# One Strassen level for the gate and up products of a decoder layer, with block sums by DMA and the hidden activations through HBM

## The reference, cut to what matters

```python
def channel_and_ple(h, p, g_ffn, w_gate, w_up, w_down, g_ple, w_ple_gate, w_ple_proj):
    n = rms_norm(h, g_ffn)
    h = h + (jax.nn.silu(n @ w_gate) * (n @ w_up)) @ w_down
    gate = jax.nn.sigmoid(rms_norm(h, g_ple) @ w_ple_gate)
    return h + gate * (p @ w_ple_proj)
```

## Time and profile before

| what | value |
|---|---|
| three timed runs | 2737.95, 2739.5, 2742.2 us; median 2739.5 |
| the profiled execution: first to last instruction | 2738.2 us |
| its own time (span plus 1.3 us, taken as the median of the runs less its span) | 2739.5 us |
| gate and up, four chunks | 255.84 + 253.70 + 253.69 + 253.70 = 1016.93 us |
| down, four chunks | 126.71 + 126.72 + 126.72 + 126.71 us |
| read through SP's DMA queue | 224.95 MB |

### The profile page before, as it was taken

How to read it: one execution, slowest core, us unless ns; L and a number is a source line. 1 busy time by engine, 2 the same in 40 slices (tenths; PEclk the granted TensorE clock), 3 DMA queues, 4 the chain that set the end, 5 groups by cost and what they waited for, 6 DMA issues and landing times. The chain is left out here.

```text
span 2738.2 us, 53856 instructions
## 1 busy us (share of the span) xinstructions
PE 2691.1 (98%) x21924; PEld 2652.9 (97%) x21924; DVE 1288.0 (47%) x1632; ACT 757.9 (28%) x1024; POOL 274.8 (10%) x279
## 2 busy tenths in 40 slices
PE   6999999999999999999999999999999999999998
PEld 6999999999999999999999999999999999999998
DVE  6557665666585553334333334333334333456332
ACT  3223332333242232222222222222222222233221
POOL 5201111111121410000000000000000000043001
PEclk8999999999999999999999999999999999999999
DMA  5733333333334323322323323333223333233332
GB/s 143 220 107 94 100 104 110 102 100 104 108 110 135 93 85 92 92 82 86 108 84 92 92 82 89 106 92 92 85 82 100 93 92 92 79 90 100 102 107 61
DMA packets 467782, 272.81 MB, mean 100 GB/s; under 512 B 17926, under 2 KB 456746, under 8 KB 467208
## 3 DMA queue, kind: packets, MB, share of 16 engines
q1 hardware_dynamic: 443216, 224.95, 28.4%
q0 software_dynamic: 20768, 43.38, 5.2%
q10 hardware_dynamic: 3744, 3.74, 0.5%
HBM read 259.11 MB, written 17.22 MB: 101 GB/s over the span
## 5 line engine op out<-in xcount | busy, mean ns | idle before, releaser
L390 PE MATMUL acc<-xhi,whi 128*128 128x260 f32 x5376 | 1103.0, 286 | 10.1 <-DVE xlo L969 7.3
L394 PE MATMUL acc<-xhi,wlo 128*128 128x260 f32 x5376 | 1089.1, 284 | 0.0
L392 PE MATMUL acc<-xlo,whi 128*128 128x260 f32 x5376 | 1087.3, 284 | 0.0
L961 DVE TENSOR_TENSOR wlo<-wraw,whi 128x1024 fp32r<-128x1024 f32 x468 | 577.4, 1234 | 968.1 <-ACT whi L705 962.2
L390 PEld LDWEIGHTS acc<-xhi,whi 128*128 128x128 f32 x5376 | 835.3, 190 | 20.1 <-DVE xlo L969 8.6
L394 PEld LDWEIGHTS acc<-xhi,wlo 128*128 128x128 f32 x5376 | 834.8, 190 | 0.0
L392 PEld LDWEIGHTS acc<-xlo,whi 128*128 128x128 f32 x5376 | 834.1, 190 | 0.0
L705 ACT ACTIVATE whi<-wraw 128x1024 fp32r<-128x1024 f32 x468 | 495.0, 1058 | 1176.4 <-PE acc L394 1093.3
L394 PE MATMUL acc<-fhi,wlo 128*128 128x260 f32 x1408 | 283.4, 283 | 0.0
L390 PE MATMUL acc<-fhi,whi 128*128 128x260 f32 x1408 | 283.3, 282 | 0.0
L392 PE MATMUL acc<-flo,whi 128*128 128x260 f32 x1408 | 283.2, 282 | 0.0
(11 more groups left out here) (214 smaller groups left out, 1489.9 us busy)
## 6 DMA issues: line engine op xcount, KB each, us to landing
wraw<-in_w_in SPq DMA_DIRECT2D x96, 512.0 KB, 3.8
wraw<-in_w_gate SPq DMA_DIRECT2D x88, 512.0 KB, 3.7
wraw<-in_w_up SPq DMA_DIRECT2D x88, 512.0 KB, 3.7
wraw<-in_w_down SPq DMA_DIRECT2D x64, 384.0 KB, 3.3
wraw<-in_w_down SPq DMA_DIRECT2D x64, 320.0 KB, 3.1
wraw<-in_w_out SPq DMA_DIRECT2D x32, 512.0 KB, 3.8
wraw<-in_w_ple_gate SPq DMA_DIRECT2D x32, 512.0 KB, 3.9
kv<-in_cache_k POOLq DMA_DIRECT2D x8, 1024.0 KB, 7.2
```

The lines of the kernel that those rows point to most:

```text
L390: mm(acc[:, slot, h, 0:HALF], w_h, hi[:, kt, h * HALF:(h + 1) * HALF], start=begin, stop=False)
L392: mm(acc[:, slot, h, 0:HALF], w_h, lo[:, kt, h * HALF:(h + 1) * HALF], start=False, stop=False)
L394: done = mm(acc[:, slot, h, 0:HALF], w_l, hi[:, kt, h * HALF:(h + 1) * HALF], start=False, stop=end)
L961: V.tensor_tensor(wlo[:, u % HILO, :], wraw[:, u % RAW, :], whi[:, u % HILO, :].bitcast(F32), ALU.subtract).then_inc(s_wlo, 1)
```

## The change

Gate and up: for a pair of hidden tiles the weight of each matrix is cut in 2x2 blocks (even or odd block of the model width, first or second hidden tile), and the data in 2x2 blocks (even or odd tile, first or second half of the tokens). Seven products of block sums (Winograd's form) take the place of eight. Each of the 44 matrix and tile-pair combinations ("pair" below, `PAIRS`) is 7 units of 24 matmuls (8 blocks by 3 matmuls, 260 columns). Of the four weight sums, DVE adds two (`block_sum`), and two are made by a DMA that POOL issues and that adds HBM data to a buffer (`add_blocks`, `accum_op`). The block buffers are single (`block_11`, `block_21`, `block_12`, `sum_1`, `sum_2`), only `block_22` is double. The seven data blocks of each of 8 tile pairs are made once (`parts_added`, `parts_hi`, `parts_lo`); those of the last four lie on the memory of the attention operand and of `hid`, so `hid` is first stored to HBM (`h_dram`). PSUM results are combined by DVE, ACT and POOL (`corner`). Each finished pair of hidden tiles is stored to HBM (`f_dram`).

Down: only after all of gate and up, in 4 passes over 4, 14, 15 and 11 hidden tiles that are loaded back (`load_hidden`); the first pass adds the stored `h_dram` tiles, which come through the two tiles of `res`. `transpose_p` moves to the last pass.

```diff
-CHUNK = 11
-CHUNKS = D_FF // P // CHUNK
-DOWN = (6, 5)
+KP2 = KT // 2
+EARLY = KP2 // 2
+FT = D_FF // P
+PAIRS = FT
+TURN = 4
+DOWN = ((4,), (7, 7), (8, 7), (6, 5))
...
@@ SP
+        def block_pair(i, first=False, last=False):
...
+                    sp.wait_ge(s_sum, i * 4 + 2 * e)
+                    sp.sem_inc(s_freed, 1)
+                block(block_21, w, 1, 0, i * (2 * P), l_21)
...
+                    sp.wait_ge(s_wlo, i * 14 + (U_G + 7 * e - 7 + 3))
+                    sp.sem_inc(s_freed, 1)
+                block(block_12, w, 0, 1, i * (2 * P), l_12)
+                if not fresh:
+                    sp.wait_ge(s_wlo, i * 14 + (U_G + 7 * e - 7 + 6))
+                    sp.sem_inc(s_freed, 1)
+                    block(block_11, w, 0, 0, i * (2 * P), l_11)
...
@@ PE
+        def gate_up(at, it, r, fresh=False):
...
+                pe.wait_ge(s_wlo, at.count(w))
...
+                to = bank(BANK_OF[u])
+                for p in range(KP2):
+                    if first and u == 0:
+                        pe.wait_ge(s_xp, p + 1)
+                    hi, lo, n = x_parts(p)
+                    w_h = whi[:, w % HILO, p * P:(p + 1) * P]
+                    w_l = wlo[:, w % HILO, p * P:(p + 1) * P]
+                    mm(to, w_h, hi[:, n, X_OF[u], :], start=p == 0, stop=False)
+                    mm(to, w_h, lo[:, n, X_OF[u], :], start=False, stop=False)
+                    done = mm(to, w_l, hi[:, n, X_OF[u], :], start=False, stop=p == KP2 - 1)
...
+        pe.wait_ge(l_f[0], 16)
...
+        with pe.Fori(1, KT // 4) as i:
+            for b in range(4):
+                pe.wait_ge(s_read, i * 4 + (T_D + b - 1))
+                unit(Span(U_D, 4, i), b, *down_units(0, 0), b % 2, True, True)
...
@@ ACT
+        def block_hi(at, it, r, v):
...
+            elif v == 5:
+                act.wait_ge(l_sum3, nn * 16 + 16)
...
+            act.wait_ge(s_unit, at.count(w) - HILO)
+            on(whi[:, w % HILO, :], source, ACT.Copy).then_inc(s_whi, 1)
...
+        def parts_hi(p):
...
+            on(hi[:, n, 0, :], hid[:, 2 * p, 0:HALF], ACT.Copy, scale=cols[:, g0:g0 + 1])
+            on(hi[:, n, 1:3, :], halves(hid[:, 2 * p + 1, :]), ACT.Copy, scale=cols[:, g0 + 1:g0 + 2])
+            act.wait_ge(s_parts, 4 * p + 4)
+            on(hi[:, n, 3:6, :], parts[p % 2][:, 0:3, :], ACT.Copy)
+            on(hi[:, n, 6, :], parts[p % 2][:, 3, :], ACT.Copy, scale=-1.0).then_inc(s_xphi, 1)
...
+        act.wait_ge(s_unit, U_G)
+        for p in range(EARLY, KP2):
+            parts_hi(p)
+            if p + 2 < KP2:
+                half_scaled(p + 2)
...
@@ DVE
+        def block_sum(at, it, r, n, fresh):
...
+            if n == 2:
+                dve.wait_ge(l_11, nn * 16 + 16)
+                dve.wait_ge(s_wlo, at.count(7 * r - 1))
+                dve.wait_ge(s_sum, it * 8 + (2 * r + 1))
+                out, a, b = sum_2, sum_1, block_11
+            V.tensor_tensor(out, a, b, ALU.add).then_inc(s_sum, 1)
...
+        def block_lo(at, r, v):
...
+            source = (block_11, sum_2, block_12, sum_1, block_22(r), block_11, sum_2)[v]
+            dve.wait_ge(s_whi, at.count(w))
...
+        def parts_added(p):
...
+            V.scalar_tensor_tensor(to[:, 1, :], hid[:, 2 * p, 0:HALF], g0, half, ALU.mult, ALU.subtract
+                                   ).then_inc(s_parts, 1)
+            V.scalar_tensor_tensor(to[:, 3, :], hid[:, 2 * p + 1, HALF:T], g1, half, ALU.mult, ALU.subtract
+                                   ).then_inc(s_parts, 1)
+            dve.wait_ge(s_parts, 4 * p + 1)
+            V.scalar_tensor_tensor(to[:, 0, :], hid[:, 2 * p + 1, HALF:T], g1, to[:, 1, :], ALU.mult, ALU.add
+                                   ).then_inc(s_parts, 1)
+            dve.wait_ge(s_parts, 4 * p + 3)
+            V.scalar_tensor_tensor(to[:, 2, :], hid[:, 2 * p + 1, 0:HALF], g1, to[:, 0, :], ALU.mult, ALU.subtract
+                                   ).then_inc(s_parts, 1)
...
+        def parts_lo(p):
...
+            V.scalar_tensor_tensor(lo[:, n, 0, :], hid[:, 2 * p, 0:HALF], g0, hi[:, n, 0, :].bitcast(F32),
+                                   ALU.mult, ALU.subtract)
+            V.scalar_tensor_tensor(lo[:, n, 1:3, :], halves(hid[:, 2 * p + 1, :]), g1, hi[:, n, 1:3, :].bitcast(F32),
+                                   ALU.mult, ALU.subtract)
+            V.tensor_tensor(lo[:, n, 3:6, :], parts[p % 2][:, 0:3, :], hi[:, n, 3:6, :].bitcast(F32), ALU.subtract)
+            V.scalar_tensor_tensor(lo[:, n, 6, :], parts[p % 2][:, 3, :], -1.0, hi[:, n, 6, :].bitcast(F32),
+                                   ALU.mult, ALU.subtract).then_inc(s_xp, 1)
...
+        for p in range(EARLY, KP2):
+            parts_lo(p)
+            if p + 2 < KP2:
+                parts_added(p + 2)
...
+                if u == 1:
+                    dve.wait_ge(s_cp, it * 8 + (2 * r + 1))
+                    if not first:
+                        dve.wait_ge(s_ev, it * 24 + 6 * r)
+                    V.tensor_tensor(v2_t, bank(X_), q1_t, ALU.subtract).then_inc(s_ev, 1)
+                if u == 3:
+                    dve.wait_ge(s_ev, it * 24 + (6 * r + 1))
+                    V.tensor_tensor(v25_t, v2_t, bank(Y_), ALU.subtract).then_inc(s_ev, 1)
...
+        def first_sum(i, b):
+            m = i * 4 + b
+            dve.wait_ge(s_unit, m + (U_D + 1))
+            dve.wait_ge(l_res[b % 2], i * 32 + (16 * (KT // 2) + b // 2 * 16 + 16))
+            V.tensor_tensor(halves(hid[:, m, :]), acc_of(b % 2), halves(res[:, b % 2, :]), ALU.add).then_inc(s_read, 1)
...
@@ POOL
+        def add_blocks(i, e, n):
...
+            to, parity, at = ((block_11, 0, l_sum3), (sum_2, 1, l_sum4))[n]
+            row = 1 - n
+            pool.wait_ge(s_wlo, i * 14 + (U_G + 7 * e + 1 + n))
...
+            pool.dma_start(to.rearrange("q (p m) -> q p m", m=P),
+                           w[:, bass.ds(i * (2 * P) + row * P, P)].rearrange("(p j q) m -> j q p m", j=2, q=P)[parity],
+                           accum_op=ALU.add).then_inc(at, 16)
...
+        def store_hidden(i, s):
+
+            pool.wait_ge(s_f, i * 3 + 3)
+            apart()
+            pool.dma_start(f_dram[:, bass.ds(i * 2, 2), 0, :], sig_t[:, :, :].bitcast(F32R)).then_inc(d_fhi, 16)
+            pool.dma_start(f_dram[:, bass.ds(i * 2, 2), 1, :], tmp[:, 2 * s:2 * s + 2, :].bitcast(F32R)
+                           ).then_inc(d_flo[s], 16)
+
+        def load_hidden(c):
+            for first, to in f_groups(c):
+                count = to.shape[1]
+                pool.dma_start(to, f_dram[:, F_CHUNK[c] + first:F_CHUNK[c] + first + count, :, :]).then_inc(l_f[c], 16)
...
+        pool.wait_ge(s_wlo, U_D)
+        pool.wait_ge(s_sum, 2 * PAIRS)
+        pool.wait_ge(d_fhi, 16 * 2)
+        pool.wait_ge(d_flo[0], 16)
+        pool.wait_ge(d_flo[1], 16)
+        load_hidden(0)
+        pool.wait_ge(d_flo[0], 16 * (PAIRS // 4))
+        for m in range(2):
+            pool.dma_start(res[:, m, :], h_dram[:, m, :]).then_inc(l_res[m], 16)
+        store_hidden(PAIRS // 2 - 1, 1)
+        pool.wait_ge(s_unit, U_D)
+        pool.wait_ge(s_ev, 6 * PAIRS)
+        pool.wait_ge(d_fhi, 16 * (PAIRS // 2))
+        pool.wait_ge(d_flo[1], 16 * (PAIRS // 4))
+        load_hidden(1)
+        for m in range(2, KT):
+            pool.wait_ge(s_read, T_D + m - 1)
+            pool.dma_start(res[:, m % 2, :], h_dram[:, m, :]).then_inc(l_res[m % 2], 16)
+        pool.wait_ge(s_read, T_D + KT)
+        load_hidden(2)
...
```

More of the change, by code:

```diff
@@ new lines, in build @@
+    up_t = sb("up_t", [P, 2, T], scope=upper)
+    upper.close()
+    after = ExitStack()
+    proj = sb("proj", [P, KT, T], scope=after)
+    after.close()
+    block_11, block_21, block_12 = (blocks[:, n, :] for n in range(3))
+    sum_1, sum_2 = wraw[:, 0, :], wraw[:, 1, :]
+    t_odd = tmp[:, 0:2, :].rearrange("p a t -> p (a t)").rearrange("p (n h) -> p n h", h=HALF)
+    parts = (t_even, t_odd)
+    q1_t, v2_t, v3_t, v25_t = (t_even[:, n, :] for n in range(4))
+    p_nat = tmp[:, 0:2, :].rearrange("p a t -> p (a t)")[:, 0:QB * D_PLE].rearrange("p (b f) -> p b f", b=QB)
@@ L374, in _, with unit @@
         mm = nc.tensor.matmul
-        def unit(at, u, hi, lo, tiles, slot, first, last, ready=None, between=None):
+        def unit(at, u, operand, tiles, slot, first, last, ready=None, between=None):
             pe.wait_ge(s_wlo, at.count(u))
@@ new lines, in hidden_hi @@
+        def hidden_hi(i, source):
+            act.wait_ge(s_f, i * 3 + 2)
+            on(sig_t[:, :, :].bitcast(F32R), source, ACT.Copy).then_inc(s_fhi, 1)
+        for r in range(TURN):
+            gate_up(Span(U_G), 0, r, fresh=True)
+        with act.Fori(1, PAIRS // TURN - 1) as it:
+            for r in range(TURN):
+                gate_up(Span(U_G, 7 * TURN, it), it, r)
+        it = PAIRS // TURN - 1
+        for r in range(TURN):
+            gate_up(Span(U_G + 7 * TURN * it), it, r, last=r == TURN - 1)
@@ new lines, in _ @@
+        dve.wait_ge(s_ninv, N_ATTN)
+        for m in range(KT):
```

(13 more changed lines are left out.)

592 lines of the change are left out of this document (407 added, 185 removed).

## The result

The changed kernel takes 2690.2 us (four runs, 2686.6 to 2692.7), the one before 2740.5 on the same chip: a ratio of 0.982, with a 95% interval of 0.980 to 0.983. Forecast were 2661 and a range of 2628 to 2755. So the sign and the range hold, and 29 us of the 79 that were expected to be gained are missing. A DMA queue's name in a row (POOLq, SPq, ACTq) is that of the engine that issued on it.

What follows compares the result with a forecast made beforehand. PE's matmul count times the distance of their starts was taken as the bound in gate and up. 2739.5 - 126.2 (matmuls) + 1.0 (transposes) + 15.3 (block start) + 28.3 (first down pass) + 3.0 (clock) = 2660.9 us; range 2628 to 2755.

Steps and rivals of the forecast that it cites:

- likeliest case: Whole kernel: the summed terms give 2660.9 us, 2651 with all ends low, 2700 with all high; chance 0.52.
- Matmuls: Gate and up: 7392 matmuls instead of 8448, 120.5 ns apart, take 890.7 us instead of 1016.9; 126.2 us saved.
- Start of the block: Gate and up's first unit: PE idles 15.3 us while DVE makes the last operand tile pairs after attention's last unit.
- First down pass: Unit 4 waits for the third h_dram tile, behind load_hidden(1)'s 7.45 MB on POOL's queue; +28.3 us.
- T: End of the last gate and up matmul; unit 4 of the first down pass starts at T + 39.9 us.
- rival 2: First down pass: the stored tiles don't stand in line behind the big load; 2633 us, chance 0.12.
- Do DVE and ACT keep up?: Gate and up, per pair of 20.24 us: DVE needs 16.8 us (83%), ACT 9.2; both fit.
- Clock: After each of two long gaps PE runs at 1.2 GHz and loses 1.5 us; 3.0 us together.
- The accumulating DMA: Gate and up's two weight sums per pair: landing 7.2 us, 3.4 us apart, costed at nothing.
- circle B: Loop of waits on `sum_2` in each gate and up pair: 16.3 us of 20.24, 3.9 us to spare.
- Rival 1: Accumulating DMA slower than its row: landing plus distance above 14.6 us costs 44 times the excess; chance 0.24.
- Rival 3: Gate and up: DVE becomes the bound of a pair if hand-overs take it past 20.24 us; 2729 us, chance 0.12.

Runs made afterwards that it cites:

- h_by_act: Against the changed kernel, ACT asks on its own queue for the first down pass's h_dram tiles from the third on, instead of POOL; 2683.6 us, ratio 0.979.
- paced: Against the changed kernel, load_hidden(2) and load_hidden(3) are cut in pieces that each wait until two more output tiles are summed; 2676.1 us, ratio 0.976.
- sq_by_act: Against the changed kernel, ACT instead of POOL makes the 16 squares of hid in the attention output, POOL only adds them; 2684.5 us, ratio 0.980.
- h_fine: Against the changed kernel, load_hidden(1) is cut in 14 pieces of 0.53 MB, one after each h_dram tile from the fourth on; 2675.4 us, ratio 0.977.
- serial_sums: Against the changed kernel, POOL asks for a pair's second accumulating DMA only when the first has landed; 2759.7 us, ratio 1.008.
- plain_loads: Against the changed kernel, each pair's two accumulating DMAs become plain loads of the same blocks, their sums left out; 2686.6 us, ratio 0.980.
- extra_adds: Against the changed kernel, POOL issues two more accumulating DMAs per pair (256 KB and 128 KB) to scratch memory, from the second pair on; 2686.2 us, ratio 0.980.

## Why the prediction was right, and where 29 us went

The forecast's likeliest case, 2651 to 2700, holds the measured time, in part by luck: its upper end was made of a slower first load, and what came instead were two stalls that stand in no term.

- **Matmuls.** Right. 890.7 us forecast; 887 us of unbroken PE from 1015 to 1902 plus the 24 matmuls before.
- **Start of the block.** Right. 15.3 forecast, 14.4 measured, in the four steps that the sum was made of; with the low clock behind it the gate and up stage is 1.0 us longer than forecast.
- **First down pass.** Right in place and cause for this kernel, and in size by luck (28.3; 3.46 + 22.23 + 0.64 = 26.3). Unit 4 starts 40.1 us after T (1942.18 - 1902.13), forecast 39.9, but two terms are off and cancel: the last hidden pair is ready for its store 11.1 us after T and not 6.8 (1913.27), and the big load and the tile behind it took 21.1 us and not 25.3 (1920.24 to 1941.35). What it said of the alternative was wrong: rival 2, tiles that do not stand in line, was priced at no stall, and h_by_act shows that the stall then passes to the weights. "Where the stall goes" was asked for the tile, not for the load beside it. The trace of before had a sign of that, in the issues of the earlier trace rows:

```profile
wraw<-in_w_in SPq DMA_DIRECT2D x3, 512.0 KB, 14.4
...
skew_dram<-bias_dram POOLq DMA_DIRECT2D x1, 512.0 KB, 14.5
```

  The `kv` load stood there behind a transfer of 512 KB too, not only behind two small ones, and SP's weight loads, on a queue of their own, took 14.4 us instead of 3.8. So this row shows company as much as a line.
- **The step that failed first**: "passes two to four have their tiles loaded during the pass before (8.0 MB, about 26 us, in 162 us), so they cost nothing". The time was enough, the company was not: the whole 8.0 MB is issued at once, and SP's loads get one tenth of the traffic; the sums that PE waits for stand behind them in DVE's list. 8.45 + 2.49 us of waits, and the clock. Shown by paced.
- **The step that was never made**: "Do DVE and ACT keep up?" was asked of a gate and up pair only. The parts of pairs 0 to 3 move into the attention output, where DVE had 50 of 92 us, and POOL's squares run there too: +7.6 us. Shown by sq_by_act.
- **Clock.** Two gaps at 1.5 us were forecast; it is three (14.4, 22.23 and 8.45 us), and each costs more. The 1.5 was itself a misreading: from 53.99 to 57.63 us stand eight entries of two matmuls, 16 and not 18, so 1.7 us were lost there. In the rows below (windows, columns as in the earlier trace rows) the granted clock is 0.50, 1.2 GHz, behind PE's 22.23 us without work; 18 matmuls take 1946.24 - 1942.18 = 4.06 us instead of 2.17. Behind the 3.46 us wait it stayed at 1.00 here; behind the same wait (3.48 us) it was 0.50 in paced, h_by_act and h_fine, 24 matmuls in 5.36 us in paced (1910.63 to 1915.99) instead of 2.89. So single runs differ by some 2.5 us in this place alone.

```profile
1914.00:1917.00 3.00, 3.00 (x25) 3.00 (x26) 1.08 (x2) 0.00 (x0) 0.73 (x1) 1.00 0.76 226
1942.00:1945.00 3.00, 2.82 (x13) 2.82 (x14) 1.26 (x3) 0.00 (x0) 1.08 (x2) 0.50 0.44 111
1945.00:1948.00 3.00, 3.00 (x22) 3.00 (x22) 0.12 (x1) 0.63 (x1) 0.00 (x0) 0.78 0.53 159
```

  Of the down stage's 45.1 us, 26.3 + 10.9 are waits and 1.0 the transposes; about 4 of the other 6.9 are this clock in two places, and some 3 stay unplaced.
- **The accumulating DMA.** Right that it costs nothing, but with far less to spare than stated. Landing and distance were 10.6 in the sum; the rows say 10.0 to 10.8 for the landing of the second, issued 1.15 us behind the first:

```profile
blocks<-in_w_up SPq DMA_DIRECT2D x85, 512.0 KB, 4.7
blocks<-in_w_gate SPq DMA_DIRECT2D x84, 512.0 KB, 5.2
blocks<-in_w_up POOLq DMA_DIRECT2D x22, 512.0 KB, 6.9
wraw<-in_w_up POOLq DMA_DIRECT2D x22, 512.0 KB, 10.8
...
blocks<-in_w_gate POOLq DMA_DIRECT2D x21, 512.0 KB, 6.4
wraw<-in_w_gate POOLq DMA_DIRECT2D x21, 512.0 KB, 10.0
```

  But the rest of circle B is 8.1 and not 5.65. In the changed kernel 11.2 us pass from the first issue to the second landing (1414.42 to 1415.57 + 10.0), so the circle has 20.24 - 11.2 - 8.1 = 0.9 us to spare, where 3.9 were forecast (a pair of `up` has 11.9 and 7.2, so 1.1). serial_sums says the same another way: 13.6 - 11.2 = 2.4 us longer, 1.58 of it paid, 0.8 free. Rival 1 would have decided at 12.1, not at 14.6. The half rate that the prediction gives beside its sum is stated by the Trainium skill ("Collectives: The Full Stack", the section on the bandwidth ceiling) for the reduce step of a ring of cores; for this DMA the packet times below give 4.2 us against 1.9.
- **Rival 3**, DVE as the bound of a pair, did not come: DVE is 79% busy in gate and up and PE waits for nothing there. PE did wait for DVE in the attention output, for another reason.

## What to carry to other kernels

When work moves into an earlier stage, add up that stage too, engine by engine, and look at which instructions of two engines will meet there. A big load that is "hidden" in a long stage can still starve the small loads that feed the stage, here on SP's and on ACT's queue: cut it, spread it by the consumer's own progress, and use the idle stretch before the stage. The margin of a circle of waits is found by adding a known delay to it; counting only the circle's own instructions forgets what else stands between them on an engine that runs its list in order.

## What the runs showed of the hardware

- A DVE instruction with two inputs in SBUF and a POOL instruction that reads SBUF hold each other up: on DVE 520 columns took 0.75 and 1.55 us, 780 columns 0.96 and 2.08, without and beside POOL; POOL's own add of 520 columns, 1.31 us, became 1.65.
- By the sum of its packets' times an accumulating DMA of 512 KB took about 4.2 us of all 16 engines, a plain load 1.9 (POOL's queue 51.5% and SP's 37.0% of 887 us, stores and other loads taken off at 1.9 per 512 KB). The forecast had 3.4 and 1.8. Its landing, 6.4 us (gate) and 6.9 (up), is only 1.2 and 2.2 above that of SP's plain loads in its company, and 1.7 and 1.5 above the plain loads that stand in its place in plain_loads (4.7 and 5.4).
- Beside one big load of POOL (7.33 MB in 301 packets), SP's loads (0.81 MB in 1614 packets) got a tenth of the bytes. That the size of the packets sets the share was not tried.
- A DMA share of 1.06 over 880 us, with PE never waiting (extra_adds).
